# Moving the last three shift rows of the second norm behind the index sums, and one key block ahead of a pool block

## What is computed

```
mod = silu(c) @ w_ada + b_ada              # shift1, scale1, gate1, shift2, scale2, gate2
h = rms_norm(x, g1) * (1 + scale1) + shift1
q, k, v, qi, ki, wi, u_pool, g_attn, g_pool = split(h @ w_in)
q, k = rms_norm(q), rms_norm(k)            # per head of 64
iscore = sum_h relu(qi_h @ ki.T) * wi_h    # causal; each query keeps its best 128 keys
attn = softmax(q @ k.T / 8 - slope * dist, selected keys) @ v
y_pool = (windowed mean(u_pool) - u_pool) @ w_grp * pool_scale @ w_pool_br
x = x + gate1 * ((sigmoid(g_attn) * (attn @ w_attn_br) + sigmoid(g_pool) * y_pool) @ w_out)
h2 = rms_norm(x, g2) * (1 + scale2) + shift2
x = x + gate2 * (silu(conv(h2 @ w_up)_a) * conv(h2 @ w_up)_b @ w_down)
```

## Time and profile before

| | |
|---|---|
| median of three runs | 734.26 us (734.16 to 734.49) |
| profiled execution, its own time | 733.26 us |
| its span | 731.4 us |
| TensorE busy | 715.4 us, 98% of the span |
| VectorE busy | 384.6 us, 53% |
| ScalarE busy | 307.1 us, 42% |
| GpSimd busy | 300.1 us, 41% |

### The profile page before, as it was taken

The page is one execution under the profiler, slowest core; times in us unless marked ns, Lnnn a source line. Parts: engine busy times, 40 slices in busy tenths (PEclk is TensorE's granted clock), DMA queues, the critical chain, the costliest instruction groups (busy, mean ns, idle before and its releaser), DMA issues.

```text
span 731.4 us, 9316 instructions
## 1 busy us (share of the span) xinstructions
PE 715.4 (98%) x3440; PEld 577.6 (79%) x3440; DVE 384.6 (53%) x706; ACT 307.1 (42%) x507; POOL 300.1 (41%) x159
## 2 busy tenths in 40 slices
PE   5899999999999999999999999999999999999997
PEld 4667688877777778887898888887888888888886
DVE  3558899965366616798855445555434432004002
ACT  6325532567577633352636344343334343121120
POOL 1001448826242325473316445444334434445340
PEclk9999999999999999999999999999999999999999
DMA  9993321311311136495095244244243233142401
GB/s 320 357 392 116 120 68 58 115 58 59 113 60 59 59 100 257 150 318 182 3 333 154 61 114 115 63 111 115 58 116 109 64 115 116 32 147 81 144 0 58
DMA packets 87306, 92.73 MB, mean 127 GB/s; under 512 B 2275, under 2 KB 69599, under 8 KB 87263
## 3 DMA queue, kind: packets, MB, share of 16 engines
q1 hardware_dynamic: 84927, 83.23, 35.6%
q10 hardware_dynamic: 2336, 8.92, 3.3%
HBM read 90.05 MB, written 2.10 MB: 126 GB/s over the span
## 4 chain that ended last, share of the span: by engine, by line
PE 83%; DVE 14%; ACT 2%; issue 1%; POOL 0%; DVEq 0%; POOLq 0%; ACTq 0%
PE bank L1592 33%; PE bank L1612 21%; PE bank L1601 17%; PE bank L1662 4%; DVE work L1329 3%; DVE top L1326 3%; PE bank L1857 1%; PE bank L1845 1%; PE bank L1824 1%; PE bank L1644 1%; PE bank L1630 1%; DVE macc_rows L1191 1%; DVE full L1507 1%; DVE pmean L1360 1%; DVE pmean L1356 1%
## 5 line engine op out<-in xcount | busy, mean ns | idle before, releaser
L721 POOL TENSOR_TENSOR wsplit<-stage,wsplit 128x1024 fp32r<-128x1024 f32 (+1 forms) x113 | 259.6, 2300 | 384.7 <-ACT wsplit L805 326.3
L1592 PE MATMUL bank<-hT,wsplit 128*128 128x512 f32 (+1 forms) x1120 | 257.4, 382 | 0.4 <-DVE hT L1515 0.4
L1592 PEld LDWEIGHTS bank<-hT,wsplit 128*128 128x128 f32 x1120 | 203.2, 188 | 41.7 <-issue 1.3
L805 ACT ACTIVATE wsplit<-stage 128x1024 fp32r<-128x1024 f32 (+2 forms) x121 | 120.1, 994 | 251.0 <-PE bank L1601 166.3
L1601 PE MATMUL bank<-hT,wsplit 128*128 128x512 f32 (+1 forms) x560 | 134.5, 382 | 0.0
L1612 PE MATMUL bank<-wsplit,guT 128*128 128x512 f32 x528 | 119.8, 389 | 0.0
L1601 PEld LDWEIGHTS bank<-hT,wsplit 128*128 128x128 f32 x560 | 101.6, 188 | 19.6 <-issue 0.2
L1612 PEld LDWEIGHTS bank<-wsplit,guT 128*128 128x128 f32 x528 | 99.1, 188 | 20.5
L1550 DVE SCALAR_TENSOR_TENSOR yb<-bank,conv,yb 128x511 f32<-128x511 f32 (+1 forms) x44 | 32.9, 749 | 65.1 <-ACT yb L1125 64.4
L1550 DVE SCALAR_TENSOR_TENSOR ya<-bank,conv,ya 128x511 f32<-128x511 f32 (+1 forms) x44 | 33.0, 749 | 59.6 <-ACT ya L1125 58.8
L1475 DVE TENSOR_TENSOR tmp_last<-bank,gate_row 128x512 f32<-128x512 f32 x8 | 5.5, 688 | 101.7 <-PE bank L1612 101.7
(11 more groups left out here) (193 smaller groups left out, 751.6 us busy)
## 6 DMA issues: line engine op xcount, KB each, us to landing
stage<-in_w_up_dram SPq DMA_DIRECT2D x44, 512.0 KB, 5.1
stage<-in_w_in_dram SPq DMA_DIRECT2D x14, 1024.0 KB, 5.2
stage<-in_w_down_dram SPq DMA_DIRECT2D x10, 1024.0 KB, 5.1
ada_first<-in_w_ada_dram SPq DMA_DIRECT2D x16, 512.0 KB, 9.1
ada_mid<-in_w_ada_dram ACTq DMA_DIRECT2D x8, 1024.0 KB, 7.8
ada_row<-in_w_ada_dram SPq DMA_DIRECT2D x8, 512.0 KB, 11.0
stage<-in_w_out_dram SPq DMA_DIRECT2D x4, 1024.0 KB, 7.0
ada_last<-in_w_ada_dram SPq DMA_DIRECT2D x4, 1024.0 KB, 10.9
```

The source lines that it names most:

```text
L721: pool.tensor_tensor(unit_split(n, 1), unit_source(n), unit_split(n, 0).bitcast(F32), ALU.subtract).then_inc(low, 1)
L805: me.did(act.activation(unit_split(n, 0), unit_source(n), ACT.Copy), high)
L1592: pe.matmul(out_bank[:, tokens], hi[:, k, :], rhs[:, part, k, tokens], start=k == 0 and part == 0, stop=False)
```

## The change

On VectorE, the shift rows of k = 5, 6, 7 leave their place behind the last block of the first norm, and come behind the last index sum, ahead of the top-8 rounds. Also on VectorE, `k_normed(1)` comes ahead of `mixed(KA - 1)`. On ScalarE, the wait ahead of the queries asks for five rows in place of all eight, and a wait for all eight comes ahead of the copies of v. No instruction is added or taken away. Lines behind the first edit have numbers that are higher by 1 to 3 in the kernel of the change (L1191 is L1192, L1368 is L1371).

```diff
--- before.py
+++ after.py
@@ -925,7 +925,7 @@
                 chunk(("gp", m))
                 me.did(act.activation(ypool[:, m, :], bank(("gp", m))[:, :], ACT.Tanh, scale=0.5), drained["act"])
 
-            act.wait_ge(mod_sum, KD)
+            act.wait_ge(mod_sum, 5)
             query(0)
             query(1)
             relus(2)
@@ -940,6 +940,7 @@
             high_parts(KD + 4)
             square_rows(0)
             high_parts(KD + 6)
+            act.wait_ge(mod_sum, KD)
             for t in range(NT):
                 v_kept(t)
             high_parts(KD + 7)
@@ -1271,7 +1272,7 @@
                 for k in (2 * q, 2 * q + 1):
                     first_low(k)
                     low_parts(k + 1)
-                for k in ((), (), (0, 1, 2, 3, 4), (5, 6, 7))[q]:
+                for k in ((), (), (0, 1, 2, 3, 4), ())[q]:
                     mod_row_of(3, k)
 
             def low_of(out_ap, full, hi, signal):
@@ -1338,6 +1339,8 @@
             query_low(3)
             for n in range(8, IH * (NT - 1)):
                 index_sum(n)
+            for k in (5, 6, 7):
+                mod_row_of(3, k)
 
             def mixed(g):
                 dve.wait_ge(part_hi, 4 + KA + g + 1)
@@ -1404,8 +1407,8 @@
                                          stat[:, 1, :].rearrange("p (t h) -> p h t", h=2 * H)[:, h, :],
                                          -slope(h), None, ALU.mult))
             k_normed(0)
+            k_normed(1)
             mixed(KA - 1)
-            k_normed(1)
             k_normed(2)
             k_normed(3)
```

## The result

| | before | after |
|---|---|---|
| median | 734.21 us (733.57 to 734.49, 4 runs) | 739.89 us (739.34 to 740.42, 4 runs) |
| ratio | | 1.0081, 95% interval 1.0069 to 1.0093 |
| span of the profiled execution | 731.4 us | 737.4 us |

The change made the kernel 5.7 us slower. I had forecast 736.8 us, slower too, with a range to 739.0; the sign held and the size did not.

The account below looks back on a forecast made before the run. Bound: TensorE, with VectorE also full between 81 and 163 us. Rows' +5.8 us shrinks to +2.8 at kroot, less 0.3 is +2.5 at the scores; on the 734.26 median, 736.8 us, range 734.3 to 739.0.

Parts of the forecast that it names:

- Part 1, kiT: Rows leaving their old place on VectorE let kiT's low part start 0.2 us earlier; the other 5.8 us become idle.
- Part 2, the rows: Rows ahead of the top-8 rounds, lengthened by mutual exclusion with GpSimd's subtraction, start the rounds 5.8 us later.
- The means: At the first two pool means, changed overlaps with GpSimd give back 0.9 and 0.5 us, leaving VectorE +4.4.
- The first of two stalls: TensorE near 135 us waits for GpSimd's late low part of the second pool block's weights and runs on at +2.3.
- The additions: The selection's last additions on VectorE meet GpSimd's gate block 1 subtraction only in part, ending at +3.2 us.
- if the last additions take 3.7 us again: Stated sign of a wrong forecast: the selection's last additions on VectorE again take 3.7 us.
- all of it arrives: Rival: means save nothing, GpSimd hits the last additions again; VectorE 5.8 us late at kroot, total 739.4; chance 0.13.
- Part 3, the key block: Second key block done in VectorE's 4.77 us idle time costs nothing and removes TensorE's 0.3 us wait at the scores.
- The sum: At the first scores, +2.8 from the kroot wait less 0.3 for the key block gives +2.5 us.

Follow-up runs that it names:

- the rows alone: Changed kernel with the key block put back behind the last mixed block, so only the shift rows and ScalarE's two waits move: 739.23 us, ratio 1.0068.
- the split: Changed kernel with one top-8 round put between the second and the third moved shift row: 738.42 us, ratio 1.0051.

## Why the prediction was wrong

*Part 1, kiT.* Right: 0.20 us earlier, idle for 4.36 us ahead of qiT. What I didn't see is that the index sums don't follow. The query's low part now waits for ScalarE (0.2 us), so that the first cap kept its place, 25.58 us from the mark in both, while GpSimd's subtraction moved 0.2 us ahead with TensorE. The cap (76.34) now came 0.1 us behind that subtraction (76.23) in place of ahead of it, and took 2.43 us in place of 0.29. Most of it fell into idle time, and the last cap ended 0.2 us later, not earlier.

*Part 2, the rows.* Right in size and in mechanism: 6.00 us for the three, GpSimd's piece stretched to 3.15. The rounds started +6.1, with +5.8 forecast; the difference is the cap.

*The means.* The savings, 0.9 and 0.5 us forecast, were 0.88 and 0.39; the product of one column that had taken 1.03 us took 0.15 (120.60). VectorE was late by 4.85 at the second mean, 4.4 forecast.

*The first of two stalls.* Here the prediction failed. It took the low part of the weights as the only thing for which TensorE waits near 135 us ("a cover of 2.1 us", "runs on at **+2.3**"). That stall came, in two pieces of 1.12 and 1.31 us (TensorE at +2.75). But the next key product writes the bank that VectorE's first mixed block empties. In the profile before, on VectorE and on TensorE:

```profile
134.35 0.74 DVE L1344 SCALAR_TENSOR_TENSOR mix<-bank,vec,mix 128x512 fp32r<-128x512 f32 x1
```

```profile
135.28 3.82 PE L1592 MATMUL bank<-hT,wsplit 128*128 128x512 f32 x16
```

The block was done at 135.1 and the product began at 135.28: a cover of 0.2 us, in no list of waits, since it was never short. The prediction had put this term at nothing. VectorE's lateness of 4.84 passed to TensorE all but whole (141.64 and 135.28 from their marks: +4.71). The experiments show it: with the first block early the wait went to the second one (done at 141.2 before, its product at 141.43), and with both early it was gone and 1.05 us came back. The edit on VectorE had the block in its queue, behind everything that I had made late, and I hadn't asked who waits for it.

*The additions.* This failed with it. With TensorE late by 4.8 and not 2.3, GpSimd's subtraction was late by the same (154.81 - 148.37 = 6.44, of which 1.65 are the mark), and met the additions just as before: 3.69 us, against 3.68 in the earlier trace rows. The saving of 1.2 us didn't come, and my own sign of being wrong did ("if the last additions take 3.7 us again"). That is one half of the rival "all of it arrives", to which I had given 0.13, at 739.4. Its other half, that the means save nothing, was wrong, and it had +5.1 at the scores where the profile has +4.4. That 739.4 lies near 739.89 is in part luck, since the clock filled the difference.

*Part 3, the key block.* Right: no wait at the scores and 0.34 us back when alone. The idle time that covered it was 4.77 us before and is 4.08 now (167.31).

*The clock.* No case had it. Behind TensorE's new waits near 140 us the granted clock fell in some executions, for 1.6 us more.

*The sum.* +2.5 forecast; +4.4 at the scores without the clock's fall; 5.6 to 5.7 in the medians. Of the 1.9 between the first two, 1.05 is the bank of the mixed blocks with what hangs on it, as measured by taking it away. The other 0.9 stood in that experiment too; it goes with VectorE and the weights being later than forecast at the second mean (+4.85 for +4.4, TensorE +2.75 for +2.3) and with the additions (+3.88 for +3.2), and no run takes these apart.

## What to carry to other kernels

When an instruction is put into a full queue, list every instruction behind it whose result or whose emptied buffer another engine waits for, and read the cover of each; the smallest decides, and a bank to be emptied counts like an input. Here two engines that were both full passed a delay on whole (0.78 of 0.79 us, 4.81 of 4.84), and work that the delayed engine did beside a third one met it again, since that one was delayed too. Look for the place where the engine is idle for other reasons: the three rows took 6.0 us in both places, and in the old one TensorE waited 0.2 us for them.

## What the runs showed of the hardware

The lower clock level behind waits was new to me. With TensorE waiting 1.1, 1.3 and 1.7 us between 130 and 142 us, the granted clock fell to 0.50 for 3.4 us (the sum over the 2 us stretches) in two of four profiles of the changed kernel, and for as long in those of the rows alone and of the split, where the first of the waits was missing and the second was 0.7; 16 matmuls took 5.5 us in place of 3.8 to 3.9. The lengths of the waits don't tell when it comes: the timed repeat of the changed kernel had 1.17, 1.35 and 1.69 us and no fall. With the last of these waits gone, moved by 6 us, or cut to 0.5 or 0.7 us, it was not seen in a profile. None of the 21 runs with a mixed block early had a mean of 0.993. That the waits cause the fall is argued from this, not shown by itself. The start has its own stretch at the lower level, near 20 us, in every kernel: 3.4 us long in four profiles, 6.8 in nine and 10.2 in one. Its length moves the whole execution, and so does a wait of TensorE for the load `ada_first`, 0.3 to 1.6 us in 8 of the 14 profiles: the marks lie from 49.11 to 52.52.

A tenth of a microsecond decides over 2 us. The first cap in the kernel before, and GpSimd's subtraction next to it:

```profile
74.69 0.29 DVE L1317 TENSOR_TENSOR iscore<-iscore,cap 128x128 f32<-128x128 f32 x1
```

```profile
74.78 2.44 POOL L721 TENSOR_TENSOR wsplit<-stage,wsplit 128x1024 fp32r<-128x1024 f32 x1 [9.63 <-ACT wsplit L805]
```

Ahead of GpSimd by 0.09 us it took 0.29; in the kernel of the change, behind it by 0.11 (76.34 and 76.23), it took 2.43.
